# A hybrid decoder trunk: the reloaded rows are added on TensorE, through products with the identity, instead of on VectorE

## Chip, core and metric

One core of a Trainium2 chip runs the whole program. The metric is device microseconds of one launch: the median of the runs, and for the reading one execution recorded by the hardware profiler. TensorE is called PE here (its weight loads PEld), VectorE DVE, ScalarE ACT, GpSimd POOL, and SyncE, which issues most transfers, SP.

## What is computed

The reference is a decoder of two layers over 512 tokens of 1024 floats. Each layer is a token mixer (NSA attention in layer 0, MLA attention in layer 1) and then a mixture of 64 experts. A router gives each token two experts and two weights. Cut to what the change touches:

```python
for i in range(2):
    x = x + mixer_i(rmsnorm(x, norm_mix[i]))
    h = rmsnorm(x, norm_ffn[i])
    # each token's two experts e0, e1 with weights w0, w1
    y = w0 * expert(h, e0) + w1 * expert(h, e1)
    x = x + y
```

with `expert(h, e) = (silu(h @ w_gate[e]) * (h @ w_up[e])) @ w_down[e]`.

## The kernel before

The tokens stand in four tiles of 128 rows. In a mixture the routed rows are sorted by expert, and PE takes one expert after the other, in blocks of 64 rows: `up` (line 1187, 16 products), a transpose of the hidden block (line 1262) and `down` (line 1196, 4 products). The weights are streamed through a ring of seven slots of SBUF, each load issued by SP when the `down` of the expert that used the slot is done. The results of experts 0 to 61 are sent by POOL to a table in DRAM (`expert_rows`). Experts 62 and 63 are kept: their results stay in SBUF (`y_sb`), and PE multiplies them by a matrix of shares, so that each tile's sum over the two kept experts builds up in two banks of PSUM (`kept_sums(t, u)`, line 1340, `u` the kept expert; each call is two products whose 64 rows of the array lie side by side).

The slots overwrite the tokens' rows x, so SP stores them to DRAM (`kept_rows`) before the mixture and loads them again near its end (line 602, semaphore `x_loaded[t]`). POOL gathers each tile's two rows per token out of `expert_rows` (line 802, semaphores `rows_landed`). DVE then puts a tile together: `add_kept(t)` adds the two banks of PSUM to the reloaded rows (line 2088), and `add_rows(t, 0)` and `add_rows(t, 1)` add the gathered rows, each times its weight (line 2078). The second of them tells `x_ready`.

The order around that is written by hand, engine by engine. PE goes through `down` of expert 63, the products of tiles 0 and 1 with it, all products of tile 2, in layer 0 the transposes of tile 0 for the next layer (`turn_tile`, line 1178, waits for `x_ready` of tile 0), and the products of tile 3. In layer 0 the MLA layer's input products follow (`latents(t)`, lines 1428 and 1433), with the transposes of the next tile between them. In layer 1 nothing follows on PE: SP stores each tile to the result when it is ready (line 679).

Of the kernel before, what the change touches and what calls it, by code (L numbers as in the profile page):

```python
# [24 lines left out]
ALU = mybir.AluOpType  # L25
# [6 lines left out]
TILES = S // P  # L32
# [90 lines left out]
def build(nc, a, out, stages):  # L123
    with ExitStack() as ctx:
# [3 lines left out]
        def sem(name):  # L128
            return ctx.enter_context(nc.semaphore(name))

        ps = ctx.enter_context(nc.psum_tensor("ps", [P, 8, 512], F32))
# [4 lines left out]
        def places(stage, first, slots=1):  # L136
            at = (SHIFT * stage + first) % SLOTS
            assert at + slots <= SLOTS
            return arena[:, at * SLOT:(at + slots) * SLOT]

        rows_of = [places(st, RING + 1, 2) for st in range(STAGES)]
        x_of = [r[:, 0:TILES * D].rearrange("p (t n) -> p t n", t=TILES) for r in rows_of]
# [4 lines left out]
        ident = identity[:, :]  # L147
# [137 lines left out]
        def y_at(stage, c):  # L285
            if c == 0:
                return hT_space_of[stage][:, 0:D]
            if c == 1:
                return places(stage, 0)[:, KD * MLA_IN:KD * MLA_IN + D]
            if c < TILES:  # L290
                return places(stage, 2)[:, (c - 1) * D:c * D]
            return h_of[stage][:, c - TILES, :]
# [113 lines left out]
        kept_done = sem("kept_done")  # L406
# [13 lines left out]
        x_loaded = [sem(f"x_loaded{t}") for t in range(TILES)]  # L420
# [77 lines left out]
        def landed(c, turn):  # L498

            return 16 * turn if c < LAST_CHUNK else 16 * (turn + (turn + 1) // 2)  # L500

        def kept_bank(t):
            return (4, 6, 2, 0)[t]
# [667 lines left out]
        def _(pe):  # L1171
            norms = [0]

            def turn_tile(rows, t):
                pe.wait_ge(x_ready, TILES + t + 1)
                for half in range(2):
                    for k in range(4):
                        last = nc.tensor.transpose(
                            ps[:, kept_bank(t) + half, k * P:(k + 1) * P],
                            rows[:, t, :].rearrange("p (m k) -> p k m", k=KD)[:, half * 4 + k, :], ident[:, :])  # L1180
                    last.then_inc(h_turned, 1)
# [60 lines left out]
            def moe_pe(l):  # L1242
                pe.wait_ge(hots_ready, 2 * l + 2)
                for c in range(TOPK * TILES):
                    last = nc.tensor.matmul(ps[:, 0, 0:CHUNKS], low_hot[:, c, :], high_hot[:, c, :],
                                            start=(c == 0), stop=(c == TOPK * TILES - 1))
# [7 lines left out]
                def up(n, c, turn):  # L1254
                    u = c % SLOTS
                    pe.wait_ge(block_ready, n + (base + 1))
                    pe.wait_ge(weights_loaded[u], (turn + (loads(u) + (PARTS[u] - 1) * (l + 1) + 1)) * 16)
                    expert(slot(l, u), x_block[:, c % 2], UP_BANKS[c % 2]).then_inc(up_done, 1)
# [11 lines left out]
                def down(n, c):  # L1270
                    turn_hidden(n)
                    finish(n, c)
# [39 lines left out]
                n = SENT - 2  # L1312
# [5 lines left out]
                n = pe.value_load(extra_n[0:1, l:l + 1], min_val=0, max_val=MAX_EXTRA)  # L1318
# [14 lines left out]
                def kept_sums(t, u):  # L1333
                    if u == 0 and t == 0:
                        pe.wait_ge(shares_ready, l + 1)
                    if t == 0:
                        pe.wait_ge(y_kept, 2 * l + u + 1)
                    for j in range(2):
                        rows = slice(j * BLOCK, (j + 1) * BLOCK)
                        last = nc.tensor.matmul(ps[:, kept_bank(t) + j, :], shares_T[rows, u, t * P:(t + 1) * P], y_sb[rows, u, :],  # L1340
                                                start=(u == 0), stop=(u == 1))
                    if u == 1:
                        last.then_inc(kept_done, 1)

                n = SENT
                up(n, n, n // SLOTS)
                pe.wait_ge(shares_made, l + 1)
# [6 lines left out]
                kept_sums(0, 0)  # L1354
                kept_sums(1, 0)
                down(n + 1, n + 1)
                kept_sums(0, 1)
                kept_sums(1, 1)
                for u in range(2):
                    kept_sums(2, u)  # L1360
                if l + 1 < LAYERS:
                    turn_tile(x_of[1], 0)
                for u in range(2):
                    kept_sums(3, u)

            def project_out(w, layer):

# [407 lines left out]
        def _(dve):  # L1775
            step = Chain(dve, dve_step)
# [195 lines left out]
            def moe_dve(l):  # L1972
# [74 lines left out]
                n = dve.value_load(extra_n[0:1, l:l + 1], min_val=0, max_val=MAX_EXTRA)  # L2047
# [14 lines left out]
                def keep_here(u):  # L2062
                    dve.wait_ge(down_done, base + SENT + u + 1)
                    if u == 0:
                        dve.wait_ge(extra_sent, l + 1)
                    dve.wait_ge(y_written[u], 16 * SENT_PAIRS * (l + 1))
                    nc.vector.tensor_copy(y_sb[:, u, :], ps[:, 2, :]).then_inc(y_kept, 1)
# [5 lines left out]
                x = x_of[l + 1]  # L2073

                def add_rows(t, k):
                    c = k * TILES + t
                    dve.wait_ge(rows_landed[c], landed(c, 2 * l + 2))
                    added = nc.vector.scalar_tensor_tensor(out=x[:, t, :], in0=y_at(l + 1, c), scalar=sent_wt[:, c:c + 1],
                                                           in1=x[:, t, :], op0=ALU.mult, op1=ALU.add)
                    if k == 0:  # L2080
                        step(added)
                    else:
                        added.then_inc(x_ready, 1)

                def add_kept(t):
                    dve.wait_ge(kept_done, l * TILES + t + 1)
                    dve.wait_ge(x_loaded[t], 16 * (l + 2))
                    step(nc.vector.tensor_tensor(x[:, t, :], x[:, t, :], ps[:, kept_bank(t):kept_bank(t) + 2, :].rearrange("p b n -> p (b n)"),
                                                 ALU.add))

                dve.wait_ge(silu_done, base + SENT + 2)
                join_hidden(1)
                keep_here(1)
                add_kept(0)
                add_rows(0, 0)
                add_rows(0, 1)
                add_kept(1)
                if l + 1 == LAYERS:
                    add_rows(1, 0)
                    add_rows(1, 1)  # L2100
                    for t in range(2, TILES):
                        add_kept(t)
                        add_rows(t, 0)
                        add_rows(t, 1)
                    return
# [3 lines left out]
                turned_half(m, 0)  # L2109
                add_rows(1, 0)  # L2110
                add_rows(1, 1)
                add_kept(2)
                add_rows(2, 0)
                add_rows(2, 1)
                turned_half(m, 1)
                add_kept(3)
                add_rows(3, 0)
                add_rows(3, 1)

# [422 lines left out]
```

## Time and profile before

| | us |
|---|---|
| median of 3 runs | 1625.5 |
| lowest and highest | 1623.71, 1628.79 |
| the profiled execution, whole | 1631.93 |
| its span, first to last instruction | 1630.2 |
| PE busy, share of the span | 1437.2 (88%) |
| DVE busy | 607.3 (37%) |
| POOL busy | 248.9 (15%) |

Two places of the program hold the lines that are changed: the end of layer 0, some 890 to 916 us into the span, with the MLA layer right behind it, and the end of the program, from some 1605 us on. The span starts at 0. In the views of the trace, busy times of PE are of records: one product of floats that fills 128 rows of the array leaves two records, one after the other, and a pair of 64-row products leaves two records side by side, twice.

### The profile page before, as it was taken

The numbers are of one execution on the slowest core, as the hardware profiler recorded it, in microseconds if no ns is written. First come the engines' busy times: TensorE is split into PE (matmuls) and PEld (weight loads), VectorE is DVE, ScalarE is ACT, GpSimd is POOL, SyncE is SP. The second block draws the span as 40 slices with busy tenths as digits, with TensorE's granted clock in tenths as the row PEclk, the third lists the DMA queues.
The fourth block names the chain that finished last, engine by engine and source line by source line (L and its number), as shares of the span: only waits on it lengthen the run. The fifth ranks groups of instructions, "written<-read, shape, count | busy, mean of one in ns | idle before, by whom it ended". The sixth has DMA issues, their size and how long they took to land.

```text
span 1630.2 us, 24202 instructions
## 1 busy us (share of the span) xinstructions
PE 1437.2 (88%) x8999; PEld 900.5 (55%) x8999; DVE 607.3 (37%) x1523; ACT 340.9 (21%) x983; POOL 248.9 (15%) x293
## 2 busy tenths in 40 slices
PE   8999999999899988787778999999899977778785
PEld 3655466655566655555555555655566655555453
DVE  2145677742532222212123556423522222222225
ACT  2122377741110000000001345412100000000000
POOL 1122100000211111111112233000211111111112
PEclk9999999999999999999999999999999999999998
DMA  7115140026699999999999401473899999999997
GB/s 294 47 52 209 50 156 1 1 119 236 240 365 430 429 429 429 429 430 430 429 430 421 184 1 78 181 297 116 340 393 426 430 429 428 429 430 430 428 430 297
DMA packets 44661, 480.91 MB, mean 295 GB/s; under 512 B 11262, under 2 KB 11790, under 8 KB 24944
## 3 DMA queue, kind: packets, MB, share of 16 engines
q1 hardware_dynamic: 28144, 450.17, 66.0%
q0 software_dynamic: 15296, 25.61, 4.5%
q10 hardware_dynamic: 1152, 4.19, 0.6%
q8 instruction: 45, 0.74, 0.2%
q14 instruction: 24, 0.20, 0.0%
HBM read 462.37 MB, written 47.19 MB: 313 GB/s over the span
## 4 chain that ended last, share of the span: by engine, by line
PE 57%; DMA 33%; DVE 6%; issue 2%; ACT 1%; another core or an unknown queue 0%; POOL 0%; SPq 0%; DVEq 0%; ACTq 0%; POOLq 0%
DMA sb_arena<-moe_w 32%; PE ps L1187 12%; PE ps L1381 7%; PE ps L1602 7%; PE ps L1196 7%; PE ps L1708 2%; PE ps L1738 2%; PE ps L1723 2%; PE ps L1568 2%; PE ps L1428 2%; PE ps L1456 2%; PE ps L1452 1%; PE ps L1288 1%; PE ps L1509 1%; PE ps L1539 1%
## 5 line engine op out<-in xcount | busy, mean ns | idle before, releaser
L1187 PE MATMUL ps<-sb_arena,sb_x_block 128*64 128x256 f32 x4096 | 473.5, 384 | 89.2 <-DMA sb_arena<-moe_w 88.7
L1187 PEld LDWEIGHTS ps<-sb_arena,sb_x_block 128*64 128x64 f32 x4096 | 419.9, 197 | 196.4 <-issue 133.5
L1196 PE MATMUL ps<-sb_arena,sb_hidden_space 128*64 128x512 f32 x1024 | 247.9, 605 | 46.0 <-ACT sb_hidden_space L918 45.6
L788 POOL DMA_INDIRECT expert_rows<-sb_y_sb,sb_row_now x124 | 133.2, 1074 | 733.0 <-DVE sb_y_sb L1984 665.7
L1983 DVE COPY sb_row_now<-sb_row_of 128x1 uint32 (+1 forms) x124 | 19.1, 154 | 601.3 <-PE ps L1196 586.8
L918 ACT COPY sb_hidden_space<-ps 128x128 f32<-128x128 f32 x128 | 34.1, 267 | 762.6 <-PE ps L1262 757.0
L1196 PEld LDWEIGHTS ps<-sb_arena,sb_hidden_space 128*64 128x64 f32 x1024 | 62.1, 136 | 143.6 <-issue 73.7
L1381 PE MATMUL ps<-sb_sorted_rows,sb_arena 128*128 128x512 f32 x256 | 114.6, 594 | 2.1 <-DVE sb_arena L2226 1.3
L1994 DVE TENSOR_TENSOR sb_x_block<-sb_sorted_rows,sb_moe_gain 128x512 f32<-128x512 f32 x120 | 83.1, 693 | 23.2 <-issue 20.7
L1984 DVE COPY sb_y_sb<-ps 128x512 f32<-128x512 f32 x124 | 84.4, 681 | 0.0
L1381 PEld LDWEIGHTS ps<-sb_sorted_rows,sb_arena 128*128 128x128 f32 x256 | 46.9, 190 | 51.4 <-issue 48.8
L1137 ACT ACTIVATE sb_arena<-ps,sb_n_max_of 128x128 f32<-128x128 f32 (+3 forms) x128 | 66.5, 527 | 13.6 <-DVE sb_n_max_of L2402 13.5
L2402 DVE TENSOR_REDUCE sb_n_max_of<-ps 128x2 f32<-128x256 f32 (+1 forms) x64 | 52.6, 823 | 33.6 <-PE ps L1710 32.2
L1602 PE MATMUL ps<-sb_sorted_rows,sb_arena 128*128 128x512 f32 x128 | 57.1, 595 | 0.0
L1602 PE MATMUL ps<-sb_arena 128*128 128x512 f32 x128 | 57.0, 593 | 0.0
L1723 PE MATMUL ps<-sb_identity,sb_arena 128*128 128x128 f32 x320 | 46.2, 275 | 8.4 <-DVE sb_arena L2412 8.1
L1708 PE MATMUL ps<-sb_arena 64*128 64x128 f32 (+3 forms) x256 | 51.8, 482 | 1.2 <-ACT sb_arena L1085 0.7
L2412 DVE TENSOR_SCALAR sb_arena<-sb_arena,sb_n_weight 128x128 f32<-128x128 f32 (+3 forms) x128 | 51.4, 443 | 2.3
L822 POOL TENSOR_SCALAR sb_rstd<-sb_ssq 128x1 f32<-128x1 f32 x6 | 1.9, 310 | 321.1 <-ACT sb_hidden_space L866 321.1
L1149 ACT COPY sb_arena<-ps 128x256 f32<-128x256 f32 (+1 forms) x64 | 44.3, 693 | 30.6 <-PE ps L1723 29.4
L914 ACT ACTIVATE sb_hidden_space<-ps 128x128 f32<-128x128 f32 x128 | 35.9, 280 | 66.8 <-PE ps L1187 63.9
L1738 PE MATMUL ps<-sb_arena 128*64 128x128 f32 x640 | 49.1, 283 | 0.3 <-ACT sb_arena L1149 0.3
(316 smaller groups left out, 1496.7 us busy)
## 6 DMA issues: line engine op xcount, KB each, us to landing
sb_arena<-moe_w SPq DMA_DIRECT2D x116, 3072.0 KB, 38.0
sb_arena<-moe_w SPq DMA_DIRECT2D x10, 2048.0 KB, 7.7
sb_arena<-moe_w SPq DMA_DIRECT2D x16, 1024.0 KB, 6.2
sb_sorted_rows<-nsa_w_group SPq DMA_DIRECT2D x2, 2048.0 KB, 13.3
sb_arena<-nsa_w_group SPq DMA_DIRECT2D x2, 2048.0 KB, 7.8
sb_sorted_rows<-nsa_w_out SPq DMA_DIRECT2D x1, 4096.0 KB, 12.1
kept_rows<-sb_arena SPq DMA_DIRECT2D x8, 512.0 KB, 4.6
token_rows<-sb_arena ACTq DMA_DIRECT2D x8, 512.0 KB, 2.6
```

The lines of the kernel that those rows point to most:

```text
L788: pool.indirect_dma_start(out=ys_dram.rearrange("r (j n) -> (r j) n", j=2), out_offset=bass.IndirectOffsetOnAxis(ap=row_now[:, u:u + 1], a ...
L1137: nc.scalar.activation(n_probs[:, s % 4, r, 0:n], ps[:, score_bank(s) + r, 0:n], ACT.Exp, bias=n_max_of[:, s % 4, r:r + 1], accum_out=n_su ...
L1187: last = nc.tensor.matmul(ps[j * BLOCK:(j + 1) * BLOCK, bank, 0:2 * P].rearrange("p (g n) -> p g n", g=2), x_rows[:, :, k], weights[:, 0:2 ...
L1196: last = nc.tensor.matmul(ps[j * BLOCK:(j + 1) * BLOCK, 2, :], hidT[:, c * BLOCK:(c + 1) * BLOCK], weights[:, 2, c * D + j * 512:c * D + ( ...
L1381: last = nc.tensor.matmul(ps[:, 4 + m % OUT_BANKS, :], hT_of[layer][:, k, t * P:(t + 1) * P], w[:, k, half * 512:(half + 1) * 512], start= ...
L1602: last = mm(ps[:, unit_bank(u), :], hT[:, k, t * P:(t + 1) * P], w[:, k, :], start=(k == 0), stop=(k == KD - 1))
L1708: mm(ps[:, bank + r, 0:n], qk_T[rows, g, c, t * P:n], qk_T[rows, g, 2 + kind, 0:n], start=True, stop=False)
L1723: last = nc.tensor.transpose(ps[:, 4 + r, j * P:(j + 1) * P], n_probs[:, s % 4, r, j * P:(j + 1) * P], ident[:, :])
L1738: last = mm(ps[r * DH:(r + 1) * DH, bank, t * P:(t + 1) * P], v_all[:, j, g, kind * DH:(kind + 1) * DH], n_probsT[:, s % 2, r, j * P:(j + ...
L1984: nc.vector.tensor_copy(y_sb[:, u, :], ps[:, 2, :]).then_inc(y_ready, 1)
L1994: return nc.vector.tensor_tensor(x_block[:, buffer].rearrange("p (a b) k -> p b a k", b=DEAL), rows.rearrange("p (b a) k -> p b a k", b=DEAL),
L2402: v.tensor_reduce(n_max_of[:, s % 4, :], ps[:, score_bank(s):score_bank(s) + 2, 0:n], AX, ALU.max, negate=True).then_inc(n_max, 1)
```

## The change

PE gets `add_rest(t)`: two products of the identity with the reloaded rows of tile t, which add them to the two banks that hold the tile's kept sums. They stand between the products of expert 62 and those of expert 63, whose last one closes the sum and tells `kept_done`. PE, and no longer DVE, waits for `x_loaded[t]`. On DVE `add_kept` is gone: `add_rows(t, 0)` reads the two banks of PSUM as its addend, after waits for the gathered rows and for `kept_done`, and writes the tile's rows; `add_rows(t, 1)` is as before.

```diff
+                def add_rest(t):
+                    pe.wait_ge(x_loaded[t], 16 * (l + 2))
+                    for j in range(2):
+                        nc.tensor.matmul(ps[:, kept_bank(t) + j, :], ident[:, :], x_of[l + 1][:, t, j * 512:(j + 1) * 512],
+                                         start=False, stop=False)
...
                 kept_sums(0, 0)
                 kept_sums(1, 0)
                 down(n + 1, n + 1)
-                kept_sums(0, 1)
-                kept_sums(1, 1)
-                for u in range(2):
-                    kept_sums(2, u)
+                for t in range(2):
+                    add_rest(t)
+                    kept_sums(t, 1)
+                kept_sums(2, 0)
+                add_rest(2)
+                kept_sums(2, 1)
                 if l + 1 < LAYERS:
                     turn_tile(x_of[1], 0)
-                for u in range(2):
-                    kept_sums(3, u)
+                kept_sums(3, 0)
+                add_rest(3)
+                kept_sums(3, 1)
...
                     dve.wait_ge(rows_landed[c], landed(c, 2 * l + 2))
+                    summed = ps[:, kept_bank(t):kept_bank(t) + 2, :].rearrange("p b n -> p (b n)")
+                    if k == 0:
+                        dve.wait_ge(kept_done, l * TILES + t + 1)
                     added = nc.vector.scalar_tensor_tensor(out=x[:, t, :], in0=y_at(l + 1, c), scalar=sent_wt[:, c:c + 1],
-                                                           in1=x[:, t, :], op0=ALU.mult, op1=ALU.add)
+                                                           in1=summed if k == 0 else x[:, t, :],
+                                                           op0=ALU.mult, op1=ALU.add)
...
-                def add_kept(t):
-                    dve.wait_ge(kept_done, l * TILES + t + 1)
-                    dve.wait_ge(x_loaded[t], 16 * (l + 2))
-                    step(nc.vector.tensor_tensor(x[:, t, :], x[:, t, :], ps[:, kept_bank(t):kept_bank(t) + 2, :].rearrange("p b n -> p (b n)"),
-                                                 ALU.add))
```

All calls of `add_kept` go with it. The order of PE's products at the end of layer 0, from expert 63's `down` to the first input products of the MLA layer, before (an `x8` counts products, not records):

```order
L1196 MATMUL ps<-sb_arena,sb_hidden_space 64x512 x4
L1340 MATMUL ps<-sb_y_sb,sb_sorted_rows 128x512 x8
L1178 MATMUL ps<-sb_identity,sb_arena 128x128 x8
L1340 MATMUL ps<-sb_y_sb,sb_sorted_rows 128x512 x4
L1428 MATMUL ps<-sb_arena 128x512 x8
```

and in the change, where line 1348 is `add_rest` and line 1437 is the old line 1428:

```order
L1196 MATMUL ps<-sb_arena,sb_hidden_space 64x512 x4
L1348 MATMUL ps<-sb_arena,sb_identity 128x512 x2
L1340 MATMUL ps<-sb_y_sb,sb_sorted_rows 128x512 x2
L1348 MATMUL ps<-sb_arena,sb_identity 128x512 x2
L1340 MATMUL ps<-sb_y_sb,sb_sorted_rows 128x512 x4
L1348 MATMUL ps<-sb_arena,sb_identity 128x512 x2
L1340 MATMUL ps<-sb_y_sb,sb_sorted_rows 128x512 x2
L1178 MATMUL ps<-sb_identity,sb_arena 128x128 x8
L1340 MATMUL ps<-sb_y_sb,sb_sorted_rows 128x512 x2
L1348 MATMUL ps<-sb_arena,sb_identity 128x512 x2
L1340 MATMUL ps<-sb_y_sb,sb_sorted_rows 128x512 x2
L1437 MATMUL ps<-sb_arena 128x512 x8
```

Eight products are new, six of them ahead of the transposes of tile 0, and the kept products now stand in five groups instead of two. At the end of the program PE's last products were, before:

```order
L1187 MATMUL ps<-sb_arena,sb_x_block 64x256 x16
L1340 MATMUL ps<-sb_y_sb,sb_sorted_rows 128x512 x4
L1262 MATMUL ps<-sb_identity,sb_hidden_space 128x128
L1196 MATMUL ps<-sb_arena,sb_hidden_space 64x512 x4
L1340 MATMUL ps<-sb_y_sb,sb_sorted_rows 128x512 x12
```

and are, in the change, from the same `down` on:

```order
L1196 MATMUL ps<-sb_arena,sb_hidden_space 64x512 x4
L1348 MATMUL ps<-sb_arena,sb_identity 128x512 x2
L1340 MATMUL ps<-sb_y_sb,sb_sorted_rows 128x512 x2
L1348 MATMUL ps<-sb_arena,sb_identity 128x512 x2
L1340 MATMUL ps<-sb_y_sb,sb_sorted_rows 128x512 x4
L1348 MATMUL ps<-sb_arena,sb_identity 128x512 x2
L1340 MATMUL ps<-sb_y_sb,sb_sorted_rows 128x512 x4
L1348 MATMUL ps<-sb_arena,sb_identity 128x512 x2
L1340 MATMUL ps<-sb_y_sb,sb_sorted_rows 128x512 x2
```

One group of twelve kept products became four groups with two identity products ahead of each. On DVE the end of layer 0 read, before (line 2067 copies expert 63's result, line 1784 copies half of a tile's transposes):

```order
L2067 COPY sb_y_sb<-ps 128x512
L2088 TENSOR_TENSOR sb_arena<-sb_arena,ps 128x1024
L2078 SCALAR_TENSOR_TENSOR sb_arena<-sb_arena,sb_sent_wt 128x1024 x2
L2088 TENSOR_TENSOR sb_arena<-sb_arena,ps 128x1024
L1784 COPY sb_arena<-ps 128x4x128
L2078 SCALAR_TENSOR_TENSOR sb_arena<-sb_arena,sb_sent_wt 128x1024 x2
```

and reads, in the change (line 2090 is the old line 2078):

```order
L2076 COPY sb_y_sb<-ps 128x512
L2090 SCALAR_TENSOR_TENSOR sb_arena<-sb_arena,sb_sent_wt,ps 128x1024
L2090 SCALAR_TENSOR_TENSOR sb_arena<-sb_arena,sb_sent_wt 128x1024
L1793 COPY sb_arena<-ps 128x4x128
L2090 SCALAR_TENSOR_TENSOR sb_arena<-sb_arena,sb_sent_wt,ps 128x1024
L2090 SCALAR_TENSOR_TENSOR sb_arena<-sb_arena,sb_sent_wt 128x1024
```

The add of each tile is gone, and the first of its two row adds reads PSUM.

## Rows read from the trace of the kernel before

**Rows 1.** The page's part 4, the chain that ended last, by engine:

```profile
PE 57%; DMA 33%; DVE 6%; issue 2%; ACT 1%; another core or an unknown queue 0%; POOL 0%; SPq 0%; DVEq 0%; ACTq 0%; POOLq 0%
```

**Rows 2.** Chain in order of time, program's end: start us, us, what:

```profile
1611.95 1.23 DVE sb_arena L2088
...
1625.84 1.28 DVE sb_arena L2078
```

**Rows 3.** Timeline of DVE, last tile: start, us, engine, line, op, tiles, count:

```profile
1623.27 1.21 DVE L2088 TENSOR_TENSOR sb_arena<-sb_arena,ps 128x1024 f32<-128x1024 f32 x1
1624.52 2.60 DVE L2078 SCALAR_TENSOR_TENSOR sb_arena<-sb_arena,sb_sent_wt 128x1024 f32<-128x1024 f32 x2
```

**Rows 4.** The page's part 6, one transfer: KB each, us to landing:

```profile
result<-sb_arena SPq DMA_DIRECT2D x4, 512.0 KB, 3.1
```

**Rows 5.** Timeline of PE, program's end (in brackets: idle before, what ended it):

```profile
1601.89 3.62 PE L1187 MATMUL ps<-sb_arena,sb_x_block 128*64 128x256 f32 x32
1605.44 1.99 PE L1340 MATMUL ps<-sb_y_sb,sb_sorted_rows 64*128 64x512 f32 x8
1607.36 0.33 PE L1262 MATMUL ps<-sb_identity,sb_hidden_space 128*128 128x128 f32 x1
1608.04 1.94 PE L1196 MATMUL ps<-sb_arena,sb_hidden_space 128*64 128x512 f32 x8 [0.36 <-ACT sb_hidden_space L918]
1610.77 5.42 PE L1340 MATMUL ps<-sb_y_sb,sb_sorted_rows 64*128 64x512 f32 x24 [0.79 <-DVE sb_y_sb L2067]
```

**Rows 6.** Timeline of PE, end of layer 0 and the MLA layer's start:

```profile
892.53 1.94 PE L1196 MATMUL ps<-sb_arena,sb_hidden_space 128*64 128x512 f32 x8 [0.35 <-ACT sb_hidden_space L918]
...
900.83 1.16 PE L1178 MATMUL ps<-sb_identity,sb_arena 128*128 128x128 f32 x8 [1.86 <-DVE sb_arena L2078]
901.91 3.42 PE L1340 MATMUL ps<-sb_y_sb,sb_sorted_rows 64*128 64x512 f32 x8
905.26 7.35 PE L1428 MATMUL ps<-sb_arena 128*128 128x512 f32 x16
912.45 1.05 PE L1178 MATMUL ps<-sb_identity,sb_arena 128*128 128x128 f32 x8
...
915.07 7.09 PE L1428 MATMUL ps<-sb_arena 128*128 128x512 f32 x16
922.00 1.04 PE L1178 MATMUL ps<-sb_identity,sb_arena 128*128 128x128 f32 x8
```

**Rows 7.** Chain in order of time, end of layer 0 and MLA's start:

```profile
901.98 3.35 PE ps L1340 x8
...
942.06 1.75 PE ps L1433 x16
```

**Rows 8.** Timeline of DVE, end of layer 0:

```profile
898.16 2.62 DVE L2078 SCALAR_TENSOR_TENSOR sb_arena<-sb_arena,sb_sent_wt 128x1024 f32<-128x1024 f32 x2 [0.49 <-issue]
```

**Rows 9.** Windows: stretch, us, busy of PE PEld DVE ACT POOL, PEclk, DMA share, GB/s:

```profile
902.00:904.00 2.00, 2.00 (x6) 0.91 (x8) 1.88 (x2) 2.00 (x4) 0.00 (x0) 0.58 1.02 403
904.00:906.00 2.00, 2.00 (x5) 0.50 (x2) 1.99 (x2) 0.61 (x2) 0.64 (x1) 0.56 0.78 315
1151.60:1158.20 6.60, 5.07 (x28) 2.62 (x30) 2.49 (x9) 0.00 (x0) 5.06 (x6) 0.50 0.94 351
1622.00:1624.00 2.00, 0.00 (x0) 0.00 (x0) 1.96 (x3) 0.00 (x0) 0.00 (x0) 0.50 0.05 18
```

**Rows 10.** Lines with shapes apart, 890 to 947 us: count, busy us, mean ns:

```profile
L2154 DVE SCALAR_TENSOR_TENSOR sb_sorted_rows<-ps,sb_mean_sq,sb_arena 128x256 f32<-128x256 f32 x8 | 3.5, 479 | 14.1 <-POOL sb_mean_sq L750 14.1
L2157 DVE SCALAR_TENSOR_TENSOR sb_sorted_rows<-ps,sb_mean_sq,sb_arena 128x64 f32<-128x64 f32 x3 | 0.8, 274 | 0.0
```

**Rows 11.** The reload of line 602: SP's timeline, and the line's times to landing:

```profile
1569.50 1.76 SPq L602 DMA_DIRECT2D sb_arena<-kept_rows x4
DMA to landing us min/median/max: 32.5/34.0/35.2
```

**Rows 12.** Waits of SP's queue: us in total, times, longest:

```profile
SPq L538 <- PE ps L1196: 672.6, 106, 7.2
```

More of the change, by code:

```diff
@@ L2093, in moe_dve @@
                 keep_here(1)
-                add_kept(0)
                 add_rows(0, 0)
                 add_rows(0, 1)
-                add_kept(1)
                 if l + 1 == LAYERS:
@@ L2101, in moe_dve @@
                     for t in range(2, TILES):
-                        add_kept(t)
                         add_rows(t, 0)
@@ L2111, in moe_dve @@
                 add_rows(1, 1)
-                add_kept(2)
                 add_rows(2, 0)
@@ L2115, in moe_dve @@
                 turned_half(m, 1)
-                add_kept(3)
                 add_rows(3, 0)
```

## The prediction

> **What bounds the kernel now.** I read the chain that ended last first: most of it is PE and transfers, DVE has 6% [rows 1]. So DVE's adds are worth something only where the chain runs through them, and I looked for the two places where the changed lines run. At the program's end the chain is DVE alone, from the first add out of PSUM at 1611.95 to the last row add, which ends at 1625.84 + 1.28 = 1627.12 [rows 2]. The reader is to see that DVE has no gap there: a tile costs one add of 1.21 and two row adds of 2.60 together [rows 3], 3.8 us, while PE was done with all kept products at 1610.77 + 5.42 = 1616.19 [rows 5]. After DVE only the last store follows, about 3.1 us [rows 4]. At the end of layer 0 it is otherwise. The chain there is PE from the kept products of tile 3 to the last input products of the MLA layer at 942.06, all of PE's work in its order [rows 7]; the row adds come into it at one point alone: PE stood 1.86 us before the transposes of tile 0, until DVE had ended that tile [rows 6].
>
> **What is removed: 1.21 us of DVE per tile, eight times.** At the program's end all four stand on the chain, 4.8 us in the best case. In layer 0 they are worth nothing. DVE's first row add began at 898.16, after an idle time of 0.49 that no engine's work ended [rows 8]; DVE's own add of tile 0 was over by then, and what is left to wait for in the code are the gathered rows. In the change the same add meets the same gathered rows, so tile 0 ends where it did, near 900.8, and the later tiles are needed only by transposes some 10 us later (912.45, 922.00, [rows 6]).
>
> **What is added: eight identity products per layer, on PE.** Such a product has 128 rows, 128 columns and 512 moving columns, as those of line 1428: 16 of their records take 922.00 - 915.07 = 6.93 us, 0.433 each [rows 6]. `add_rest` is two products, four records: 1.73 us. A call of `kept_sums` is four records of another shape (64 rows, two side by side): the block of 24 lasts 5.42 and the block of 8 lasts 1.99, so 3.43 / 16 = 0.214 a record [rows 5], 0.86 us a call. An identity product does the work of one DVE add of half a tile, but costs twice a kept product.
>
> **What is moved: PE changes its shape much more often.** The block of eight kept records at 1605.44 should hand over after 8 x 0.214 = 1.71; the transpose behind it, whose input was long there, starts after 1.92 [rows 5]. That is 0.21 for the two changes around a block, and what the block's own first record came late is not in it. I take 0.15 for one change; the ends are 0 (PE hides it, as it hides weight loads of one shape) and 0.2. Beside this row stands a rule of the Trainium skill that speaks against the change: TensorEngine Tiling (Array Packing), section Tiling Modes, Key Properties, says that a change of tiling mode drains TensorE. As an estimate from that rule, with a drain of what the last pair of `down` outlasts its turn (1.94 - 8 x 0.214 = 0.23 us, [rows 5]), each change would cost 0.23 and the sum of all below would be +3.7 instead of +2.2.
>
> **Sum, end of layer 0.** PE is free of expert 63's `down` at 892.53 + 8 x 0.214 = 894.24 [rows 5, 6]. Then come, without any wait, four `add_rest` (6.92), six calls of `kept_sums` (5.16), the transposes (900.83 to 901.91 with one change, so 0.93, [rows 6]) and eleven changes of shape (1.65): the MLA products start at 908.90, where they started at 905.26. The wait for expert 63's copy (0.79 of idle in the like place, [rows 5]) and the 1.86 us before the transposes are filled, but with more than they held: the transposes would start near 903.9, after tile 0 is ready. Their readers have time: DVE's and ACT's copies of them end well before 908.9. That is 3.64 late. Against it stands the clock. Between 902 and 906 the granted clock was 0.58 and 0.56, that is mostly the lower level, 1.2 GHz, and rose again by itself; the eight kept records there took 3.42 instead of 1.99, and the first MLA block 912.45 - 905.26 = 7.19 instead of 6.93 [rows 5, 6, 9]. It fell right after PE's 1.86 us of idle. In the change PE has no idle there, and I take the higher level throughout, which gives back 0.26 behind 905.26 (what it gives back before that is already in the sum). Layer 0: **+3.4 us**; with the ends of the price of a change, +1.7 and +3.9. It reaches the program's end one for one, since everything behind is started by it: PE goes on without a gap to 942.06 [rows 7], and later the weight loads wait for PE's `down` 106 times [rows 12].
>
> **Sum, the program's end.** `down` frees PE at 1608.04 + 1.71 = 1609.75. Four `add_rest`, six calls of `kept_sums` and eight changes (1.20) end at 1623.03; from a call's end to DVE's start it is 1611.95 - 1610.77 - 0.86 = 0.32 [rows 2, 5], so DVE starts the last tile at 1623.35. It needs 2.60 and ends at 1625.95, against 1627.12: **-1.2 us**, with ends -2.4 and -0.8. So PE takes over the bound from DVE: tile 0 starts at 1613.0, a microsecond later than before, tile 1 at 1615.9, tile 2 at 1619.6, tile 3 at 1623.35, and DVE stands about 1 us before each of the last two. The row add out of PSUM is not in this trace. An add of that size out of PSUM takes 1.21 and the row add without PSUM 1.30 [rows 3]; a scalar-tensor-tensor out of PSUM grows from 274 ns at 64 columns to 479 at 256, 1.07 ns a column, which would be 1.30 at 1024 [rows 10]. I take 1.30; the lower end is worth 0.1 at the last tile.
>
> Two waits move with this. PE now waits for the reload, with all kept products queued behind it. It is issued from 1569.50 in 1.76 us and lands at most 35.2 later, by 1606.5; PE asks at 1609.9 [rows 11]. So it costs nothing, and each microsecond that it came over 3.4 later would be one of the result. And DVE asks earlier for the last gathered rows, at about 1624.7 instead of 1625.8: the transfers were quiet from 1622 on, which leaves these rows over 2 us [rows 9].
>
> **Sum of all:** +3.4 - 1.2 = +2.2 us. Against the profiled execution, 1631.93, that is 1634.1. The median of the runs is 6.4 below that execution; taken over, the forecast is 1627.7. With the ends of the price of a change the net is -0.7 to +3.1.
>
> **Rivals.** *The clock falls all the same, and the result is slower.* For it: near the start of layer 1's experts there is a stretch of 6.6 us at 0.50 although PE was busy in 5.07 of it [rows 9], so a fall needs no long idle time. Against it: in the change nothing interrupts PE from 892.5 to 908.9. Its price in layer 0: 6.6 us at half speed are 3.3 us, net +5.5, time 1631.0. It decides from 5.4 us at the lower level on, where the net passes 4.9. *Changes of shape cost nothing.* For it: within one shape the weight loads are hidden. Against it: the 0.21 [rows 5]. Net -0.7, time 1624.8. *Layer 0's delay is swallowed later.* For it: a third of the chain is transfers [rows 1], which might start on their own time. Against it: they wait for PE [rows 12]. Then the end alone counts: -1.2, time 1624.3. *The reload comes too late for PE*, and the change trades a DVE add for a PE wait: slower by each microsecond over the 3.4.
>
> **How the numbers follow.** A measurement of this kernel can tell about 0.3%, 4.9 us, from no change. Forecast 0.65; changes free 0.15; delay swallowed 0.10; clock 0.08; reload late 0.02. Predicted is the forecast's 1627.7. The range goes from under the swallowed delay, by half of what the three runs lie below their median, 1623.3, to a little over the clock case, 1631.5. Faster by over 0.3% would need 4.9, more than DVE's whole 4.8: 0.03. Slower by over 0.3% are the clock, the reload and a little of the forecast's upper side: 0.10. Within 0.3%: 0.87.
>
> **What will show it.** In the profile after: identity records at 0.43 each, 16 of them a layer, no idle of PE from expert 63's `down` to the MLA products; those starting 3 to 4 us later after that `down` than before (12.7 before, 16.4 predicted); a granted clock of 1.00 there; at the end DVE waiting for PE before tiles 2 and 3, and 16.2 instead of 17.4 from PE's free time to DVE's end. Wrong would make it: records of the identity products at another pace, a wait of PE for the reload, the delay of layer 0 gone before the experts' last block, or a DVE row add out of PSUM far from 1.30.

## The result and the profile after

| | before | after |
|---|---|---|
| median of 7 runs, us | 1626.25 | 1632.9 |
| lowest and highest, us | 1623.71, 1629.3 | 1630.38, 1634.86 |
| profiled execution, us | 1631.93 | 1632.9 |
| its span, us | 1630.2 | 1630.7 |

The ratio of the runs is 1.0031, with an interval of 1.0017 to 1.0046: slower, by an amount that lies right at the bound of 0.3%. The forecast was 1627.7. The median of 1632.9 lies 1.4 us above the end of its range, 1631.5; by the ratio, on the median of before that the forecast stood on, it is 1625.5 x 1.0031 = 1630.5, which lies inside. The two profiled executions differ by 1 us and the medians by 6.65. That is the first thing to explain: the profiled execution after took the median of its runs, and the one before, 1631.93, took longer than the slowest of its seven, 1629.3. So it may not stand for its kernel.

The page of the kernel after, its parts 1 and 4 (busy us by engine; shares of the chain that ended last):

```profile
PE 1451.7 (89%) x9031; PEld 904.4 (55%) x9031; DVE 598.1 (37%) x1515; ACT 340.9 (21%) x983; POOL 246.4 (15%) x293
PE 60%; DMA 33%; DVE 4%; ACT 1%; issue 1%; POOL 0%; SPq 0%; DVEq 0%; ACTq 0%; POOLq 0%
```

Beside [rows 1], the chain has moved from DVE to PE, as the change moves the work. DVE is busy 9.2 us less and PE 14.5 more; the sixteen identity products are 32 records of 0.433, 13.9 us.

**End of layer 0.** PE's timeline of the kernel after, which answers to [rows 6]:

```profile
892.12 1.94 PE L1196 MATMUL ps<-sb_arena,sb_hidden_space 128*64 128x512 f32 x8 [0.35 <-ACT sb_hidden_space L918]
893.99 1.98 PE L1348 MATMUL ps<-sb_arena,sb_identity 128*128 128x512 f32 x4
895.90 1.13 PE L1340 MATMUL ps<-sb_y_sb,sb_sorted_rows 64*128 64x512 f32 x4
896.96 1.98 PE L1348 MATMUL ps<-sb_arena,sb_identity 128*128 128x512 f32 x4
...
903.77 1.16 PE L1178 MATMUL ps<-sb_identity,sb_arena 128*128 128x128 f32 x8
...
907.83 1.13 PE L1340 MATMUL ps<-sb_y_sb,sb_sorted_rows 64*128 64x512 f32 x4
908.89 7.13 PE L1437 MATMUL ps<-sb_arena 128*128 128x512 f32 x16
915.86 1.04 PE L1178 MATMUL ps<-sb_identity,sb_arena 128*128 128x128 f32 x8
```

No row from 893.99 on has a bracket: PE waits for neither the reload nor DVE. The MLA products start 908.89 - 892.12 = 16.77 after expert 63's `down`. An identity block takes 1.91 from its start to the next (895.90 - 893.99), of which four records of 0.433 are 1.73: 0.18 go into the change of shape. A kept call behind it takes 1.06 (896.96 - 895.90), of which 0.86 are its records: 0.20 for the change back. DVE's timeline there, which answers to [rows 8]:

```profile
897.62 1.28 DVE L2090 SCALAR_TENSOR_TENSOR sb_arena<-sb_arena,sb_sent_wt,ps 128x1024 f32<-128x1024 f32 x1 [2.82 <-DMA sb_arena<-expert_rows,sb_pos_u]
898.98 1.29 DVE L2090 SCALAR_TENSOR_TENSOR sb_arena<-sb_arena,sb_sent_wt 128x1024 f32<-128x1024 f32 x1
```

The first row add waits for the gathered rows, here by name, and the transposes find tile 0 ready.

**End of the program.** PE's timeline, which answers to [rows 5]:

```profile
1609.44 1.94 PE L1196 MATMUL ps<-sb_arena,sb_hidden_space 128*64 128x512 f32 x8 [0.36 <-ACT sb_hidden_space L918]
1611.31 1.98 PE L1348 MATMUL ps<-sb_arena,sb_identity 128*128 128x512 f32 x4
...
1623.86 1.13 PE L1340 MATMUL ps<-sb_y_sb,sb_sorted_rows 64*128 64x512 f32 x4
```

and DVE's, which answers to [rows 3]:

```profile
1614.48 1.28 DVE L2090 SCALAR_TENSOR_TENSOR sb_arena<-sb_arena,sb_sent_wt,ps 128x1024 f32<-128x1024 f32 x1 [2.36 <-PE ps L1340]
...
1621.28 1.28 DVE L2090 SCALAR_TENSOR_TENSOR sb_arena<-sb_arena,sb_sent_wt,ps 128x1024 f32<-128x1024 f32 x1 [1.23 <-PE ps L1340]
...
1625.11 1.28 DVE L2090 SCALAR_TENSOR_TENSOR sb_arena<-sb_arena,sb_sent_wt,ps 128x1024 f32<-128x1024 f32 x1 [1.23 <-PE ps L1340]
1626.43 1.28 DVE L2090 SCALAR_TENSOR_TENSOR sb_arena<-sb_arena,sb_sent_wt 128x1024 f32<-128x1024 f32 x1
```

PE is the bound now: DVE stands 1.23 us before each of the last two tiles. From the start of `down` to DVE's end it is 1627.71 - 1609.44 = 18.27, against 1627.12 - 1608.04 = 19.08 before: 0.8 us gained.

By these two places alone, layer 0 lost 16.77 - 12.73 = 4.0 and the end gave back 0.8, net 3.2. The two spans differ by no more than 0.5 because the profiled execution after is shorter in places that the change doesn't touch: 0.4 ahead of expert 63's `down` of layer 0 and 2.0 between the output projection and layer 1's second expert. Another 0.2 lies in the first MLA products, 6.97 us here and 7.19 in [rows 6]. Neither the 0.5 nor the 3.2 is the 6.65 of the medians.

### The profile page after: what moved, and what is told of

It is laid out like the page before. It is cut to its first block, busy times and chain, and to the rows that moved or that the text cites. A ratio compares the mean times of both kernels' runs of the same rounds, so it can differ in the third digit from the quotient of the medians.

```text
span 1630.7 us, 24250 instructions
## 1 busy us (share of the span) xinstructions
PE 1451.7 (89%) x9031; PEld 904.4 (55%) x9031; DVE 598.1 (37%) x1515; ACT 340.9 (21%) x983; POOL 246.4 (15%) x293
## 4 chain that ended last, share of the span: by engine, by line
PE 60%; DMA 33%; DVE 4%; ACT 1%; issue 1%; POOL 0%; SPq 0%; DVEq 0%; ACTq 0%; POOLq 0%
DMA sb_arena<-moe_w 32%; PE ps L1187 12%; PE ps L1390 7%; PE ps L1196 7%; PE ps L1611 7%; PE ps L1717 2%; PE ps L1747 2%; PE ps L1732 2%; PE ps L1577 2%; PE ps L1437 2%; PE ps L1465 2%; PE ps L1461 1%; PE ps L1288 1%; PE ps L1518 1%; PE ps L1548 1%; PE ps L1645 1%
## 5 line engine op out<-in xcount | busy, mean ns | idle before, releaser
L1992 DVE COPY sb_row_now<-sb_row_of 128x1 uint32 (+1 forms) x124 | 19.1, 154 | 601.3 <-PE ps L1196 582.4
```

## The experiments

The runs below stand beside runs of the kernel before of their own. The ratio is that of the runs with a 95% interval; 0.001 is 1.6 us. Four stage lengths, read from the profile of each run, carry the argument (us):

- A: layer 0, from expert 63's `down` to the first MLA input product
- B: MLA attention, from the last product of line 1452 (1461 in the kernel after) to the first of the output projection (line 1381, or 1390)
- C: layer 1, from the second expert's `down` to the third's
- D: the program's end, from expert 63's `down` to DVE's last add

| kernel | A | B | C | D | span | ratio, interval |
|---|---|---|---|---|---|---|
| before, the profile of the prediction | 12.7 | 70.8 | 9.5 | 19.1 | 1630.2 | |
| e5_before_again | 11.2 | 69.2 | 11.2 | 19.1 | 1627.0 | 0.9998 (0.9986 to 1.0011) |
| after | 16.8 | 70.7 | 9.5 | 18.3 | 1630.7 | 1.0031 (1.0017 to 1.0046) |
| e3_change_again | 16.8 | 70.8 | 11.2 | 18.3 | 1632.4 | 1.0048 (1.0036 to 1.0061) |
| e6_change_third | 16.8 | 70.7 | 11.2 | 18.3 | 1634.5 | 1.0031 (1.0020 to 1.0043) |
| e2_layer0_only | 16.8 | 70.7 | 9.5 | 19.1 | 1631.6 | 1.0042 (1.0029 to 1.0055) |
| e1_end_only | 11.3 | 69.2 | 11.2 | 18.3 | 1625.6 | 0.9999 (0.9989 to 1.0009) |
| e4_grouped | 16.7 | 70.8 | 11.2 | 19.1 | 1635.3 | 1.0034 (1.0021 to 1.0047) |
| e8_end_tiles23 | 11.1 | 69.1 | 9.5 | 16.6 | 1622.4 | 0.9979 (0.9966 to 0.9991) |
| e7_best | 10.3 | 69.2 | 9.5 | 16.6 | 1620.7 | 0.9973 (0.9962 to 0.9984) |
| e9_delay4 | 14.7 | 69.1 | 11.2 | 19.1 | 1630.9 | 1.0022 (1.0010 to 1.0033) |
| e10_delay6 | 16.3 | 70.7 | 9.5 | 19.1 | 1631.6 | 1.0037 (1.0024 to 1.0050) |
| e11_delay8 | 18.0 | 69.2 | 9.5 | 19.1 | 1630.2 | 1.0044 (1.0031 to 1.0057) |
| e12_change_delay2 | 18.5 | 69.2 | 11.2 | 18.3 | 1633.9 | 1.0045 (1.0032 to 1.0058) |

C is 9.5 in seven profiles and 11.2 in seven, and differs between executions of one code (before and e5, after and e3), so it is kept out of the comparisons. In the seven with 11.2 the granted clock (PEclk in the windows; 1.00 is 2.4 GHz, 0.50 is 1.2) falls once more at that place, 1170 to 1179 us into the span; in the others it doesn't. From the output projection to the last `down` the three profiles of the kernel after take 536.9, 540.2 and 540.8 us: the span of a single profile can't price the change.

### One layer at a time

The change is made for a list of tiles per layer, and a tile that is not in it keeps DVE's add. This is e1's list; e2 has the two halves exchanged:

```diff
+        REST = ((), (0, 1, 2, 3))
...
                 def add_rest(t):
+                    if t not in REST[l]:
+                        return
...
+                    from_ps = k == 0 and t in REST[l]
...
                 def add_kept(t):
+                    if t in REST[l]:
+                        return
```

> The change in layer 1 alone; the end of layer 0 is as before. Theory (two places, no others): from the start of expert 63's down to DVE's last row add 18.3 us instead of 19.1, the MLA products of layer 1 start 12.7 us after that down as before; time 0.8 us under the kernel before, ratio 0.9995. Rival (the change costs some 2 us more somewhere outside the two places, whichever layer it stands in): ratio 1.000 to 1.001.

> The change in layer 0 alone; the program's end is as before. Theory: first MLA products 16.8 us after the start of expert 63's down instead of 12.7, the transposes of tile 1 23.7 instead of 19.9, granted clock 1.00 there; the end 19.1 as before; time 3.8 us over the kernel before, ratio 1.0023. Rival (some 2 us more outside the two places): ratio 1.0035.

> The changed kernel once more, for a narrower interval. Theory: +3.8 in layer 0 and -0.8 at the end, +3.0 us, ratio 1.0018. Rival (2 us more outside the two places): +5 us, ratio 1.0031 as first measured.

The change at the end alone measures 0.9999: its 0.8 us lie inside the interval, and the profile shows them, D being 18.3. The change in layer 0 alone measures 1.0042, 6.8 us. So all of the loss is made by layer 0, and it is larger than the 3.4 forecast. The kernel after, run anew, gives 1.0048. The theory of the two places, priced against the trace of before, missed in e2 and e3 (1.0023 and 1.0018 were expected). And e1 brings something that was not looked for: its layer 0 is the code of before, and takes 11.3 us there, not 12.7.

### The kernel before again

No edit: the kernel before and the kernel after, each run as a change against before.

> The kernel before, run as if it were a change. Its profile is a second look at the end of layer 0. Theory (the clock falls there in some executions of this kernel only, and the profiled one was such): either 11.3 us from expert 63's down to the first MLA products with a granted clock of 1.00, or 12.7 with a stretch at 0.50; ratio 1.0000, which also shows what a null comparison gives. Rival (the 12.7 is the rule, and the 11.3 seen in the kernel with the change at the end alone is an accident): 12.7.

> The changed kernel a third time. Theory (layer 0 costs 5.5 us against an execution without a fall of the clock and 3.8 against one with it; the end gives back 0.8): +3.0 to +4.7 us, ratio 1.0018 to 1.0029. Rival (1.5 to 3 us more elsewhere): ratio 1.0038 to 1.0048. Its own layer 0 again 16.8 us at a granted clock of 1.00.

The null run gives 0.9998, and the kernel after 1.0031 again, between the theory's 1.0029 and the rival's 1.0038; its interval holds both. The profile of the null run differs from that of before where it matters. PE's timeline of e5, end of layer 0, to be held against [rows 6]:

```profile
891.26 1.94 PE L1196 MATMUL ps<-sb_arena,sb_hidden_space 128*64 128x512 f32 x8 [0.35 <-ACT sb_hidden_space L918]
893.99 3.70 PE L1340 MATMUL ps<-sb_y_sb,sb_sorted_rows 64*128 64x512 f32 x16 [0.79 <-DVE sb_y_sb L2067]
899.50 1.16 PE L1178 MATMUL ps<-sb_identity,sb_arena 128*128 128x128 f32 x8 [1.81 <-DVE sb_arena L2078]
900.59 1.99 PE L1340 MATMUL ps<-sb_y_sb,sb_sorted_rows 64*128 64x512 f32 x8
902.51 7.13 PE L1428 MATMUL ps<-sb_arena 128*128 128x512 f32 x16
```

Its windows (stretch, us, busy of PE PEld DVE ACT POOL, PEclk, DMA share, GB/s), two in this place and two at MLA attention:

```profile
900.00:904.00 4.00, 4.00 (x18) 1.93 (x18) 3.77 (x5) 3.16 (x6) 1.05 (x2) 1.00 1.01 398
904.00:908.00 4.00, 4.00 (x11) 1.80 (x10) 3.67 (x3) 0.00 (x0) 0.02 (x1) 1.00 0.36 147
...
1000.00:1004.00 4.00, 2.26 (x16) 1.51 (x15) 3.68 (x15) 1.68 (x8) 1.59 (x2) 1.00 0.02 4
1004.00:1008.00 4.00, 4.00 (x23) 2.26 (x22) 2.04 (x5) 2.20 (x8) 0.00 (x0) 1.00 0.46 131
```

PE idles before the transposes as long as in [rows 6], 1.81 against 1.86, and yet the clock stays at its higher level, 2.4 GHz: the eight kept records behind take 1.99 and not 3.42, and A is 902.51 - 891.26 = 11.25 and not 12.73. So the fall that [rows 9] show at 902 to 906 does not come with the code: of four profiles with this layer 0 (before, e1, e5 and e8) one has it, though PE's idle time there is 1.69 to 1.89 us in all four.

The second difference is B. The kernel after at MLA attention, the same view:

```profile
1004.00:1008.00 4.00, 2.35 (x17) 1.44 (x15) 3.00 (x12) 1.90 (x7) 2.03 (x3) 1.00 0.01 4
1008.00:1012.00 4.00, 3.81 (x16) 2.36 (x17) 2.13 (x9) 1.60 (x7) 0.07 (x1) 0.61 0.00 0
```

Here the clock is at 0.61 in the four microseconds in which PE starts again behind a wait for DVE; e5 shows 1.00 behind the same wait. One group of products tells what it costs, in PE's timeline of the kernel after:

```profile
1008.19 0.63 PE L1479 MATMUL ps<-sb_identity,sb_sorted_rows 128*128 128x128 f32 x4 [1.74 <-DVE sb_sorted_rows L2209]
1008.65 0.27 PE L1480 MATMUL ps<-sb_identity,sb_sorted_rows 128*128 128x128 f32 x1
1008.76 1.78 PE L1518 MATMUL ps<-sb_arena 128*128 128x256 f32 x4
```

and in that of e5 (line 1509 is 1518 there):

```profile
1001.81 0.63 PE L1470 MATMUL ps<-sb_identity,sb_sorted_rows 128*128 128x128 f32 x4 [1.74 <-DVE sb_sorted_rows L2207]
1002.27 0.27 PE L1471 MATMUL ps<-sb_identity,sb_sorted_rows 128*128 128x128 f32 x1
1002.38 1.03 PE L1509 MATMUL ps<-sb_arena 128*128 128x256 f32 x4
```

The same wait of 1.74, the same products, 1.78 against 1.03. Over the stage it is 70.7 against 69.2, 1.5 to 1.6 us. All five profiles with the change in layer 0 have it (after, e2, e3, e6, and e4 with its other order, below); of the four with the layer 0 of before, only the one that the prediction was made from. That execution had both falls, 1.5 us in A and 1.6 in B, which e5, e1 and e8 have not.

### Fewer changes of shape

Against the kernel after: in both layers the identity products of two tiles stand together, then the kept products of two tiles, so that six changes fewer lie ahead of the MLA products. Tile 3's stand ahead of the transposes too:

```diff
                 down(n + 1, n + 1)
                 for t in range(2):
                     add_rest(t)
+                for t in range(2):
                     kept_sums(t, 1)
-                kept_sums(2, 0)
-                add_rest(2)
-                kept_sums(2, 1)
+                for t in (2, 3):
+                    kept_sums(t, 0)
+                for t in (2, 3):
+                    add_rest(t)
+                for t in (2, 3):
+                    kept_sums(t, 1)
                 if l + 1 < LAYERS:
                     turn_tile(x_of[1], 0)
-                kept_sums(3, 0)
-                add_rest(3)
-                kept_sums(3, 1)
```

> The same identity and kept products, put in groups of one shape, so that PE changes its shape 5 times instead of 11 at the end of layer 0 and 4 instead of 8 at the program's end; the products of tile 3 also stand ahead of the transposes of tile 0. Theory (a change costs 0.19 us): the MLA products start 15.6 to 15.9 us after expert 63's down (16.8 in the change), and the end gets longer by 1 us, since tiles 2 and 3 are ready at almost the same time: 19.1 to 19.4 from that down to DVE's last add; whole time 0 to 0.3 us under the changed kernel. Rival (changes of shape are free and the excess lies in the products themselves): 16.8 in layer 0.

PE's timeline of e4, end of layer 0:

```profile
894.52 3.70 PE L1349 MATMUL ps<-sb_arena,sb_identity 128*128 128x512 f32 x8
898.15 3.70 PE L1341 MATMUL ps<-sb_y_sb,sb_sorted_rows 64*128 64x512 f32 x16
901.78 3.70 PE L1349 MATMUL ps<-sb_arena,sb_identity 128*128 128x512 f32 x8
905.41 1.99 PE L1341 MATMUL ps<-sb_y_sb,sb_sorted_rows 64*128 64x512 f32 x8
907.33 1.16 PE L1179 MATMUL ps<-sb_identity,sb_arena 128*128 128x128 f32 x8
909.32 7.11 PE L1439 MATMUL ps<-sb_arena 128*128 128x512 f32 x16 [0.83 <-ACT sb_arena L846]
```

In the trace the last transpose starts at 908.22, and one follows the other by 0.11, so PE could go on at 908.33, 13.81 us after the first identity product; the kernel after needs 908.89 - 893.99 = 14.90 for the same products. Six changes less give 1.09, 0.18 each, which agrees with the 0.18 and 0.20 above. The time does not get it: with nothing between the transposes and the MLA products PE waits for ACT's copy of the transposes (0.83 by the bracket, which counts from the end that the profile gives the last one), and A is 16.7, where 15.6 to 15.9 was expected. At the end D is 19.1 again, for DVE gets its first tile later. The ratio, 1.0034, can't be told from that of the kernel after. So changes of shape cost about a fifth of a microsecond each, and here the order that saves them opens waits instead.

### Is it the moment or the products?

Against the kernel before: layer 0's code, with products of the identity with itself (0.87 us each, their result is not used) behind the transposes, lengthens layer 0 and adds nothing else. They are made by `keep_busy`, a helper that the kernel before has at other places. There are four in e9, as here, six in e10 and eight in e11; e12 is the kernel after with two of them in the same place:

```diff
                 if l + 1 < LAYERS:
                     turn_tile(x_of[1], 0)
+                    keep_busy(4)
```

> The kernel before with four products of the identity with itself (3.5 us of PE) between the transposes of tile 0 and the products of tile 3, nothing of the change. Theory (the 1.6 us that came on top in every longer layer 0 are a fall of the clock at the start of the MLA layer's attention, and whether it comes depends on the moment at which this start is reached, not on the change's products): first MLA products 14.8 us after expert 63's down; from the last unit's first product to the output projection 69.2 us, no fall; +3.5 us, ratio 1.0021. Rival (any longer layer 0 brings the fall): 70.8, ratio 1.0031.

> The same with six such products, 5.2 us, nearly the 5.5 that the change adds. Theory: 16.5 us to the first MLA products, the fall is there as with the change, 70.8 us; +6.8 us, ratio 1.0042. Rival (the fall needs the change's own products): 69.2, +5.2 us, ratio 1.0032.

> The same with eight such products, 6.9 us. Theory: 18.2 us to the first MLA products, no fall, 69.2 us; +6.9 us, ratio 1.0042, no more than with six. Rival (any longer layer 0 brings the fall): 70.8, +8.5 us, ratio 1.0052.

> The changed kernel with two such products more, 1.7 us, at the same place. Theory: 18.5 us to the first MLA products, but no fall behind them, 69.2 instead of 70.7: the time of the changed kernel, within 0.5 us of +6.3, ratio 1.0039. Rival (the fall belongs to the change): 70.7, +8 us, ratio 1.0049.

With six, A is 16.3, nearly that of the kernel after, and B is 70.7. With four and eight, A is 14.7 and 18.0, and B is 69.1 and 69.2. PE's timeline of e10 at MLA attention:

```profile
1008.15 0.63 PE L1471 MATMUL ps<-sb_identity,sb_sorted_rows 128*128 128x128 f32 x4 [1.73 <-DVE sb_sorted_rows L2208]
...
1008.72 1.72 PE L1510 MATMUL ps<-sb_arena 128*128 128x256 f32 x4
```

and of e11, the same products behind the same wait:

```profile
1008.23 0.63 PE L1471 MATMUL ps<-sb_identity,sb_sorted_rows 128*128 128x128 f32 x4 [1.74 <-DVE sb_sorted_rows L2208]
...
1008.81 1.03 PE L1510 MATMUL ps<-sb_arena 128*128 128x256 f32 x4
```

So the fall doesn't need the products of the change: a delay without any of them brings it, and the profile before had it without a delay. Nor do these products force it: e12, the kernel after with 1.7 us more work, has none. That the length of layer 0 decides, and not the single execution, rests on one profile of each of e9 to e12. The traces hold something to set them against: an earlier fall of the clock, whose start lies 433.1 to 435.9 us into the span in all fourteen profiles. Counted from that start, the products behind the wait in B begin after (us):

| profiles | from the first fall | fall at B |
|---|---|---|
| e7, e8, e5, e1 | 566.8, 567.0, 568.0, 568.1 | no |
| before | 570.1 | yes |
| e9 | 571.2 | no |
| e10, after, e6, e2, e3, e4 | 572.7, 572.7, 572.8, 573.1, 573.2, 573.5 | yes |
| e11, e12 | 574.3, 574.6 | no |

In this order no profile stands among those of the other kind. In time from the span's start they do: e10's products begin at 1008.15 and have the fall, e11's at 1008.23 and have none. The five profiles with the change lie within 0.8 us of each other, so the code ahead of B seems to set this distance, and the change to have moved it by some 5 us, to where the fall comes. The profile before stands behind e5 and e1 by 2.0 us, of which its fall in A makes 1.5. This order was found afterwards, and no run was made to test it.

The times alone don't show the fall in B. A and B together (e9 +3.5, e10 +5.1 +1.5, e11 +6.8) give 1.0022, 1.0041 and 1.0042, near the measured ratios, but the interval of e10 holds its time with and without the fall. That of e12 holds the 1.0039 expected and its rival's 1.0049.

### What the end can give, and a kernel that beats both

Tiles 0 and 1 of layer 1 keep DVE's add, and only tiles 2 and 3 get theirs from PE; layer 0 is that of before. Beside e1 only the list differs:

```diff
+        REST = ((), (2, 3))
```

> The reloaded rows of tiles 2 and 3 at the program's end alone go through PE, all else as before. Theory (DVE bound for tiles 0 and 1, PE's work hidden behind it): the end 16.7 us instead of 19.1, layer 0 at 11.3 or 12.7 as the clock falls or not; 2.4 us under the kernel before, ratio 0.9985. Rival (DVE waits for PE all the same): the end 18.3, ratio 0.9995.

DVE's timeline of e8, the program's end:

```profile
1606.69 1.22 DVE L2106 TENSOR_TENSOR sb_arena<-sb_arena,ps 128x1024 f32<-128x1024 f32 x1 [1.23 <-PE ps L1341]
1607.95 2.60 DVE L2094 SCALAR_TENSOR_TENSOR sb_arena<-sb_arena,sb_sent_wt 128x1024 f32<-128x1024 f32 x2
...
1614.24 1.27 DVE L2094 SCALAR_TENSOR_TENSOR sb_arena<-sb_arena,sb_sent_wt,ps 128x1024 f32<-128x1024 f32 x1
...
1616.75 1.27 DVE L2094 SCALAR_TENSOR_TENSOR sb_arena<-sb_arena,sb_sent_wt,ps 128x1024 f32<-128x1024 f32 x1
```

DVE starts on tile 0 as early as before and has no gap to its end: PE computes the sums of tiles 2 and 3 while DVE works on tiles 0 and 1. Two adds of 1.21 are gone from the path, and D is 16.6, 2.5 less than before; the ratio is 0.9979.

The last kernel adds to that, in layer 0, the kept products of tile 3 ahead of the transposes, where PE waited 1.81 us for DVE; and ACT copies its half of the transposes between its scalings of the weights (line 969), since that copy would be late next. Against e8:

```diff
-                kept_sums(2, 0)
-                add_rest(2)
-                kept_sums(2, 1)
+                for t in (2, 3):
+                    kept_sums(t, 0)
+                    add_rest(t)
+                    kept_sums(t, 1)
                 if l + 1 < LAYERS:
                     turn_tile(x_of[1], 0)
-                kept_sums(3, 0)
-                add_rest(3)
-                kept_sums(3, 1)
...
                 for t in range(TILES):
-                    turn_copy(t)
+                    if t > 0:
+                        turn_copy(t)
...
                     nc.scalar.activation(w_in[:, k, :], w_in[:, k, :], ACT.Copy, scale=mix_gain[:, 1, k:k + 1]).then_inc(w_in_scaled, 1)
+                    if k == 4:
+                        turned_half(turns[0], 0)
```

> At the program's end the reloaded rows of tiles 2 and 3 alone go through PE; in layer 0 all adds stay on DVE, tile 3's kept products stand ahead of tile 0's transposes, where PE was idle, and ACT copies its half of these transposes after five of its eight scalings of the MLA weights instead of after all. Theory: first MLA products 10.3 us after expert 63's down (11.3 or 12.7 before), DVE's last add 16.7 us after that down at the end (19.1 before): 3.4 to 4.8 us under the kernel before, ratio 0.9970 to 0.9979. Rival (the delay of layer 0 or the end does not reach the time): ratio 0.999 to 1.000.

PE's timeline of e7, end of layer 0:

```profile
893.86 5.42 PE L1344 MATMUL ps<-sb_y_sb,sb_sorted_rows 64*128 64x512 f32 x24 [0.79 <-DVE sb_y_sb L2080]
899.35 1.16 PE L1182 MATMUL ps<-sb_identity,sb_arena 128*128 128x128 f32 x8
901.41 7.11 PE L1441 MATMUL ps<-sb_arena 128*128 128x512 f32 x16 [0.90 <-ACT sb_arena L846]
```

The wait before the transposes is filled, a wait of 0.90 for ACT's copy opens behind them, and A is 10.3 instead of 11.2. Its median is 1623.8 us and its ratio 0.9973: 4.4 us faster than before, with an interval of 2.6 to 6.2, so it beats both kernels, as e8 does. What it has over e8, 0.9 us in A, is less than the runs can tell; the profile alone shows it.

## Why the prediction was right in part and wrong in part

The measured cost of the change is 6.0 us (the mean of the ratios 1.0031, 1.0048 and 1.0031, of 1626), and the forecast had +2.2. By the stages it is +5.5 (A, 16.8 against 11.3) + 1.6 (B) - 0.8 (D) = +6.3, a ratio of 1.0039, which all three intervals hold; without B it would be 1.0029, which two of them hold. That the first ratio puts the time inside the range is luck: the range went up to 1631.5 for a fall of the clock at the end of layer 0, and none came there. Point by point:

- **The mechanism in layer 0 was right.** PE bounds it, the adds that DVE loses there are worth nothing, the MLA products start 16.77 us after `down` (16.4 predicted), nothing interrupts PE, and the clock does not fall there: between its falls at 435 and 1008.9 it is 1.00. The delay arrives at the end of the program; *the delay is swallowed* fell with e2, *the reload comes too late* with the timeline after.
- **The first step that failed is what the delay was measured from.** The prediction read 12.7 us in its trace, saw that the clock fell there, and tied that to PE's 1.86 us of idle, as if it came with the code; the change would have taken it away and earned the difference. Three other profiles of the same code (e1, e5, e8) have the idle time and no fall. The +3.4 was 3.64 - 0.26. Without the fall, the kept products are 1.43 us shorter and there is no 0.26 to earn: 3.64 + 1.43 = 5.1. The sign was at hand: [rows 5] and [rows 6] hold the same eight kept products at 1.99 and at 3.42, and the profiled execution was 6.4 us above the median. Of these 6.4, 3.1 are the falls in A and B; the prediction carried all of them over as if they had nothing to do with the stages that it compared.
- **The price of a change of shape was mis-sized.** 0.15 was taken, with 0.2 as the upper end; 0.18 and 0.20 were measured. At their mean of 0.19 eleven of them make the 0.4 us between 5.1 and 5.5. *Changes cost nothing* is out. The Trainium skill, TensorEngine Tiling (Array Packing), section Tiling Modes, Key Properties, says that a change of tiling mode drains TensorE. The trace agrees that such a change costs time, 0.18 and 0.20 us; that it is a drain no run shows. The prediction's estimate from that rule, 0.23, missed the 0.19 by as much as the 0.15 that was taken.
- **The second step that failed is the clock behind the change.** The sum looked for falls only where PE's work was changed. The lengthened layer 0 moves all that comes after it, and in all five profiles with the change a fall at MLA attention comes with that, 1.6 us. The rival of a falling clock named a net of +5.5 and so came nearest in size, but put the fall into layer 0, so that its nearness is luck. What was brought up for it was misread, too: [rows 9] show the stretch at 0.50 from 1151.6 on, behind the start of the fall, and not what PE did ahead of it. From 1148.0 to 1151.5 PE was busy 0.85 us, and it stood 3.80 for a transfer, as PE's timeline of before has it:

```profile
1152.66 1.15 PE L1288 MATMUL ps<-sb_identity,sb_sorted_rows 64*128 64x64 f32 x16 [3.80 <-DMA sb_sorted_rows<-token_rows,sb_token_pair]
```

That a fall can come behind a shorter wait is shown by B, 1.74 us.

- **At the end, -1.2 was forecast and -0.8 measured.** PE took over the bound as predicted, DVE stands 1.23 before each of the last two tiles, and the row add out of PSUM takes 1.28 (1.30 taken). The missing 0.3 to 0.4 are the eight changes of shape, 1.5 instead of 1.2, and 0.07 more from a call to DVE's start (1625.11 - 1623.86 = 1.25).

The bound between no change and slower was set at 4.9 us. The net of 6.0 to 6.3 lies past it, on the side that was given 0.10.

**What stays open:** why the clock falls behind one and the same wait at one moment and not at another. The delays and the table of distances from the first fall speak for the moment; they don't show why some distances have the fall and others not. Nor was it settled how many of the unprofiled runs of before and after have these falls.

## What to carry to other kernels

Before a stage's length from one profile goes into a sum, see whether the granted clock fell in it, price the stage at either level from rows of the same instructions, and don't let a change earn the difference unless more than one execution shows the fall. When work goes from one engine to another at the end of a program, move only as much as the other engine can do in the shadow of the first: four tiles' adds on TensorE gained 0.8 us at the end, two of them 2.5. And saved changes of shape or filled waits are worth only what the next wait behind them leaves, as the 0.83 and 0.90 us for ACT's copy showed.

## What the runs showed of the hardware

- The granted clock behind the same idle time of PE and ahead of the same products was 1.00 in one execution and about 0.6 in the next, and a delay of layer 0 by 5.1 us brought a fall 100 us later that delays of 3.5 and 6.8 us did not (one profile each).
- A change between fp32 products of 128 rows and pairs of 64 rows cost 0.18 us one way and 0.20 back, and an order with six changes less saved 0.18 for each.
- A scalar-tensor-tensor of 128x1024 floats takes 1.28 us with its addend in PSUM and 1.28 with it in SBUF: on DVE, reading the sum out of PSUM cost nothing.
